# Where the moving operands of the weight products begin in SBUF

## The reference

```
def reference(x, mem, ...):
    x = first_block(x, mem, ...)     # norm @ w_in; pool, rwkv7, differential attention; @ w_out;
                                     # cross-attention to mem; conv FFN 1024 -> 2*2816 -> 1024
    x = second_block(x, ...)         # norm @ w_in; gated spatial unit, top-k attention; merged @ w_o;
                                     # FFN 1024 -> 4096 -> 1024
    return third_block(x, ...)       # 16 meta tokens; norm @ w_in; forgetting attention, gated delta
                                     # rule; @ w_out; conv FFN 1024 -> 2*2816 -> 1024
```

## Time and profile before

| | |
|---|---|
| time, median of 3 runs | 2923.33 us (2919.9 to 2925.94) |
| profiled execution: span from the first to the last instruction | 2921.2 us |
| PE busy | 2791.6 us (96%), 16646 matmul instructions |
| PEld (weight loads) busy | 2339.7 us (80%) |
| DVE (VectorE) busy | 1603.6 us (55%) |
| ACT (ScalarE) busy | 1047.6 us (36%) |
| POOL (GpSimd) busy | 616.9 us (21%) |
| mean granted TensorE clock | 0.974 of full |

### The profile page before, as it was taken

The page is one execution under the profiler, slowest core; times in us unless marked ns, Lnnn a source line. Parts: engine busy times, 40 slices in busy tenths (PEclk is TensorE's granted clock), DMA queues, the critical chain, the costliest instruction groups (busy, mean ns, idle before and its releaser), DMA issues. The chain is left out here.

```text
span 2921.2 us, 42543 instructions
## 1 busy us (share of the span) xinstructions
PE 2791.6 (96%) x16646; PEld 2339.7 (80%) x16646; DVE 1603.6 (55%) x2432; ACT 1047.6 (36%) x1786; POOL 616.9 (21%) x495
## 2 busy tenths in 40 slices
PE   8989999999999999998999999999888998999998
PEld 6769876878888766857788888986777898999986
DVE  5865556365553464934433336975443455576643
ACT  4354343432222323252423224546343233422223
POOL 3430110221100121440100003345454000121101
PEclk9989899999999999989999999999999999999999
DMA  4200221122223321202222222210000122222231
GB/s 157 89 8 8 94 94 58 56 90 94 94 94 98 108 65 66 94 8 80 95 94 94 94 94 73 88 51 2 6 2 1 51 89 78 76 99 92 90 98 61
DMA packets 60307, 210.62 MB, mean 72 GB/s; under 512 B 7926, under 2 KB 8566, under 8 KB 59990
## 3 DMA queue, kind: packets, MB, share of 16 engines
q1 hardware_dynamic: 58934, 207.39, 21.4%
q10 hardware_dynamic: 1184, 0.59, 0.1%
HBM read 205.84 MB, written 2.10 MB: 71 GB/s over the span
## 5 line engine op out<-in xcount | busy, mean ns | idle before, releaser
L272 PE MATMUL ps<-normed_hi,slab_hi 128*128 128x264 f32 (+2 forms) x2568 | 868.6, 338 | 28.0 <-DVE normed_lo L576 13.6
L274 PE MATMUL ps<-normed_hi,slab_lo 128*128 128x264 f32 (+2 forms) x2568 | 852.1, 332 | 0.0
L273 PE MATMUL ps<-normed_lo,slab_hi 128*128 128x264 f32 (+2 forms) x2568 | 851.0, 331 | 0.0
L153 ACT ACTIVATE slab_hi<-ring 128x1024 fp32r<-128x1024 f32 x376 | 397.2, 1057 | 964.3 <-PE ps L274 951.8
L157 DVE TENSOR_TENSOR slab_lo<-ring,slab_hi 128x1024 fp32r<-128x1024 f32 x360 | 479.4, 1334 | 385.0 <-ACT slab_hi L153 384.5
L272 PEld LDWEIGHTS ps<-normed_hi,slab_hi 128*128 128x128 f32 x2568 | 486.0, 189 | 96.4 <-issue 35.0
L273 PEld LDWEIGHTS ps<-normed_lo,slab_hi 128*128 128x128 f32 x2568 | 486.4, 189 | 52.2 <-issue 4.3
L274 PEld LDWEIGHTS ps<-normed_hi,slab_lo 128*128 128x128 f32 x2568 | 484.6, 189 | 49.1
L272 PE MATMUL ps<-hidden_hi,slab_hi 128*128 128x512 f32 x560 | 221.0, 395 | 5.6 <-DVE hidden_lo L223 5.6
L274 PE MATMUL ps<-hidden_hi,slab_lo 128*128 128x512 f32 x560 | 223.0, 398 | 0.0
L273 PE MATMUL ps<-hidden_lo,slab_hi 128*128 128x512 f32 x560 | 221.0, 395 | 0.0
(11 more groups left out here) (579 smaller groups left out, 3951.9 us busy)
## 6 DMA issues: line engine op xcount, KB each, us to landing
ring<-in_stream SPq DMA_DIRECT2D x376, 512.0 KB, 3.3
h<-in_x SPq DMA_DIRECT2D x8, 256.0 KB, 5.8
mix_y<-in_sgu_b SPq DMA_DIRECT2D x1, 1024.0 KB, 6.3
out_features<-ffn_hidden SPq DMA_DIRECT2D x2, 512.0 KB, 3.2
xn<-in_c_recip_count SPq DMA_DIRECT2D x1, 512.0 KB, 3.2
rwkv_a<-in_mem SPq DMA_DIRECT2D x1, 512.0 KB, 4.0
rwkv_b<-in_mem SPq DMA_DIRECT2D x1, 512.0 KB, 4.9
sgu_ln<-in_sgu_ln SPq DMA_DIRECT2D x1, 512.0 KB, 7.8
```

The costliest lines, as they stand in the source:

```text
L153: self.nc.scalar.activation(self.hi[:, n % PARTS, :], self.ring[:, n % SLOTS, :], ACT.Copy).then_inc(self.hi_ready, 1)
L272: nc.tensor.matmul(to, lhsT[0], rhs[0], start=start, stop=False)
L273: nc.tensor.matmul(to, lhsT[0], rhs[1], start=False, stop=False)
L274: return nc.tensor.matmul(to, lhsT[1], rhs[0], start=False, stop=stop)
```

## The change

No instruction is added, taken out or reordered; each engine's program has the same instructions and waits in the same order. What changes is where operands lie. The two parts of an activation are now cut out of one tensor by `spaces`, which adds as many unused bytes in front as are needed to begin at a given place modulo 256. `moving` picks it: 0 for rows of up to 512 columns, and 224 with 576 words (2304 bytes, nine times 256) per row for rows of 528. So all 5832 matmuls of 512 columns that move `normed`, `rows` or `hidden` begin at 0, as the 192 of 256 columns did already; the 5040 of 264 columns begin at 224 (first half) and 0 (second half, since 224 + 1056 is 1280). The last FFN keeps its 512-column rows in the same space, 8 words further, which is 0 again. The 384 that move a slab still begin at 128; their weights (`normed`) began at 160 or 0 and now begin at 0. The small table `gdn_keep` no longer has a buffer, it lies in a part of `wide_v` that is free at the time. Buffers that are opened behind the enlarged ones lie some bytes further.

```diff
+BOUNDARY, WORD = 256, 32
+OPERAND_AT = 0
+WIDE_AT, WIDE = 224, 576
+HIDDEN_AT = (OPERAND_AT - WIDE_AT) % BOUNDARY // 4
...
-        self.hi, self.lo = at or (K.buf(ctx, f"rows_{n}", [P, parts] + shape, F32R) for n in ("hi", "lo"))
+        self.hi, self.lo = at or K.moving(ctx, "rows", [parts] + shape)
...
+    def spaces(self, ctx, name, at, words):
+        self.count += 1
+        skipped = (at - -(-self.nc.sbuf_base // WORD) * WORD) % BOUNDARY
+        both = ctx.enter_context(self.nc.sbuf_tensor(f"{name}_{self.count}", [P, skipped // 4 + 2 * words], F32R))
+        return [both[:, skipped // 4 + n * words:skipped // 4 + (n + 1) * words] for n in range(2)]
+
+    def moving(self, ctx, name, shape):
+        at, pitch = (OPERAND_AT, shape[-1]) if shape[-1] <= S else (WIDE_AT, WIDE)
+        return [laid(x, shape, pitch) for x in self.spaces(ctx, name, at, math.prod(shape[:-1]) * pitch)]
+
+def laid(space, shape, pitch):
+    rows = space[:, 0:math.prod(shape[:-1]) * pitch].rearrange("p (r n) -> p r n", n=pitch)[:, :, 0:shape[-1]]
+    return rows if len(shape) == 2 else rows.rearrange("p (a b) n -> p a b n", b=shape[1])
...
-        self.hi, self.lo = (K.buf(ctx, f"normed_{name}", [P, KT, n], F32R) for name in ("hi", "lo"))
+        self.hi, self.lo = K.moving(ctx, "normed", [KT, n])
...
-        parts = [K.buf(local, f"rows_{x}", [P, PARTS, S], F32R) for x in ("hi", "lo")]
+        parts = K.moving(local, "rows", [PARTS, S])
...
-        parts = [K.buf(local, f"hidden_{x}", [P, PARTS, S], F32R) for x in ("hi", "lo")]
+        parts = K.moving(local, "hidden", [PARTS, S])
...
-        wide_parts = [K.buf(local, f"rows_{x}", [P, PARTS, 2, T3], F32R) for x in ("hi", "lo")]
-        out3 = Residual3(K, K.xn, rows, wide_parts)
-        ffn = Ffn(K, local, "ffn3", rows, 2 * FT, FT, [x[:].rearrange("p n k t -> p n (k t)")[:, :, 0:S] for x in wide_parts])
+        spaces = K.spaces(local, "rows", WIDE_AT, PARTS * 2 * WIDE)
+        out3 = Residual3(K, K.xn, rows, [laid(x, [PARTS, 2, T3], WIDE) for x in spaces])
+        ffn = Ffn(K, local, "ffn3", rows, 2 * FT, FT, [laid(x, [PARTS, HIDDEN_AT + S], 2 * WIDE)[:, :, HIDDEN_AT:] for x in spaces])
...
+        keep = wide_v[0:8, 1, :]
...
-            keep = K.buf(fox, "gdn_keep", [8, T3])
```

More of the change, by code:

```diff
@@ L2 @@
 from contextlib import ExitStack, contextmanager
+import math
 import numpy as np
@@ L2901, in __init__ @@
         self.K, self.gains = K, gains
-        parts = [K.buf(ctx, f"hidden_{x}", [P, PARTS, S], F32R) for x in ("hi", "lo")]
+        parts = K.moving(ctx, "hidden", [PARTS, S])
         rows = Rows(K, ctx, "norm2_g_2", S)
@@ L3066, in decays, with mix_in_3_stage @@
         nc.scalar.activation(heads[:, 1, :], heads[:, 1, :], ACT.Sigmoid)
-def mix_in_3_stage(K, network, fq, fk, fv, gin, wide_heads, keep, causal, scale, factor, ins):
+def mix_in_3_stage(K, network, fq, fk, fv, gin, wide_heads, causal, scale, factor, ins):
     nc = K.nc
@@ L4113, in block_3 @@
             fv = K.buf(fox, "fox_v", [P, NC3, 512])
-            mix_in_3_stage(K, network, fq, fk, fv, gin, wide_heads, keep[:], causal, scale[:], factor[:], ins)
+            mix_in_3_stage(K, network, fq, fk, fv, gin, wide_heads, causal, scale[:], factor[:], ins)
             K.h, K.xn = normed, fq
```

## The result

The changed kernel takes 2936.0 us (median of 5 runs, 2931.26 to 2937.07) against 2923.89 us for the one before: the ratio is 1.0044, with a 95% interval of 1.0032 to 1.0056. It is 12 us slower, where 43 us less were forecast and 2837 to 2918 us were allowed for.

The account below looks back on a forecast made before the run. TensorE was taken as the bound, through the distance between back-to-back products. Savings of 40.5 us (512 columns) and 6 us (264 columns), less 3 us for waits, gave 43.5 us off 2923.3: 2880 us, range 2837 to 2918.

Parts of the forecast that it names:

- The bound and the method: TensorE's back-to-back products set the time; distance per product is window length over the matmul count less two.
- That starts modulo 256 matter: Products of 512 columns: 229 ns from 192, 233 from 160 or 224, so the start costs at least 4 ns.
- 512 columns at 0: Products moving `normed`, `rows`, `hidden`: 225.2 ns each from start 0 (bounds 213.3 to 237.0), saving 40.5 us.
- the boundary is the bad place: Rival: moving start's phase against the weights' start decides; at 237.0 ns from 0, 2945 us; chance 0.07.
- The reason given for 225.2 within the bounds: Weight load gives the surcharge a fixed part, since 264 columns pay 10.8 ns and 512 pay 16 to 20.
- that 256 columns do not foretell: Sign of a wrong prediction: 512 columns from 0 have a price not foretold by 256 columns (118.5 ns).
- 264 columns at 224 and 0: The 5040 half-row products gain 1.2 ns each from the fixed pair of starts, 6 us (−4 to 13).
- The allowance of 3 us for a cover gone: VectorE, feeding slabs and draining PSUM, would be 93 and 94% busy in two stretches; a few waits cost 3 us.
- The 384 products with a moving slab: Moving start stays at 128, weights move to 0; put at 0, 1.5 us either way at 4 ns.
- The rule of the Trainium skill: Warm matmuls follow after N / 2.4 GHz plus about 2.5 ns, through two independent read ports; the change gives 0 us.
- The 215.8 ns of the prediction: The skill pages' distance for 512 columns at any start; if the new start brought it, 92 us instead of 40.5.

Follow-up runs that it names:

- fourth kernel: Kernel before with 512-column operands at 0, but single tensors at 32, 64, 96, 128, 160 or 208 modulo 256, wide rows unmoved; 2906.70 us in one run.

## Why the prediction was wrong

**The bound and the method were right.** TensorE sets the end, no cover was missing, and the loss is in the distance between products. The time of every kernel above follows from those distances to within some 8 us, part of which goes with the granted clock. That starts modulo 256 matter was right too: 229 and 233 ns did belong to the starts (the kernel with all at 192).

**The step that failed: "512 columns at 0".** "If 256 more columns from a boundary add only their own 106.7 ns, 512 columns from 0 take 118.5 + 106.7 = 225.2 ns." They take 232.7. In this term 40.5 us were forecast, and the balance of the 512-column products is nil (the kernel with 512 columns at 0, 0.9985). The error has two parts. The row of 256 columns was no guide to the effect of a start: such products stayed near 119 ns whatever their start was. As means from start to start they took 119.1 ns at 0 with weights at 128, and 119.6 both at 128 with weights at 128 and at 0 with weights at 0, so equal starts even cost half a nanosecond. (That the weight loads, 112 ns, hold them there is likely, but no run shows it.) And I took the boundary of 256 bytes as the thing to be at. What the rows showed was only that two starts out of four seen were cheaper or dearer; every product of before had the same start of weights, so its part could not be seen. That part was named in the rival "the boundary is the bad place" (the phase against weights that begin at 128), with a chance of 0.07. That mechanism, the moving start against the weights' start, is what the runs found, though its price at 0 was 232.7 and not 237.0 ns, just under the 233.1 from which that rival would have decided. The reason given for 225.2 within the bounds, that the weight load makes a fixed part of the surcharge, was not borne out either: loading a half or a quarter of the weight columns left 229.6 to 231.8 ns. The prediction had named the sign, a price of 512 columns from 0 "that 256 columns do not foretell", and it came.

**The second step that failed: "264 columns at 224 and 0".** The pair was timed inside a sequence in which the halves rotate through eight starts, 0.72 us for six. Standing alone, the same pair takes 0.74; it went from the cheapest six of the rotation to a price that none of them had. 6 us of gain were forecast, with bounds of −4 to 13; 11.5 us of loss came. The bounds took in only the rounding of the rows, not that a product's distance depends on what runs ahead of it. The kernel with only the low weights shifted shows the same thing for 512 columns.

**The terms put at little or nothing.** The allowance of 3 us for a cover gone was not called on; nothing got faster. The 384 products with a moving slab, put at 0, went from 233.2 to 232.8 ns in the first stage (means from start to start), which is nothing. With `normed` at 128, where the slab begins, the same products took 228.4 ns: equal starts help with the roles exchanged as well. With the three terms put right, 2880 + 40.5 + 6 + 11.5 − 3 is 2935 us.

**The rule of the Trainium skill** ("TensorE: Matmul & The Clock Gate", "Step-by-step: what each phase is for") that the moving operand and the weights come through ports that do not slow each other disagrees with these runs: the same moving operands take 227.0 or 231.4 ns, depending on where the low part of the weights begins. The 215.8 ns of the prediction were not seen at any start; the least was 226.7. For this change, though, its verdict of no gain was nearer than mine.

**What stays open.** Why equal starts are best, why 192 (64 past the weights) comes second and 128 apart is as slow as 32 apart, and what the 13 ns over the streaming time at equal starts are. They are not the columns loaded, and they are absent at half clock: 213 ns for 256 columns, and 426.9 ns for 512, again 512 / 1.2 GHz, as the mean of eleven distances of the kernel before. Halves of 264 columns that both begin at the weights' start were not tried, since a row of 528 would have to be split in memory.

## What to carry to other kernels

Where float32r products of 512 columns stand back to back, each with a weight load of its own, put the moving operand and the weights at the same address modulo 256. Here that made 233.3 ns into 226.7, and the kernel 1.3% faster than before (2888 against 2924 us). About 29 us of these 36 follow from the distances, by an estimate (6.6 ns for the 4392 products that were at 160, 224 or 64, 2.2 ns for the 912 that were at 192, less the share at half clock). The rest goes with a granted clock of 0.976 to 0.978 in three of its four runs, where the runs of the kernel before had 0.972 to 0.974; the one at 0.973 took 2896 us. For 256 and 264 columns hardly anything was to be had. Judge a start by a long window in which nothing else stands, never by one product in a mixture of starts. And before you extrapolate from rows that differ in one address, ask what all of them have in common: a quantity that never varies in a trace has its effect hidden in every row.

## What the runs showed of the hardware

Products of 512 columns at full clock, by the moving operand's start minus the weights' start, modulo 256; each number is a mean of the distances from start to start over one stage (the fourth kernel is the one with six other starts):

```
difference  ns            read in
0           226.7         hidden, both blocks, weights at 128 and moving at 128; the same with both at 0
32          233.3         kernel before, normed of block 1
64          228.9, 233.3  all operands at 192; rows of block 1 with only the wide rows moved
80          231.2         fourth kernel, normed of block 2 at 208
96          233.3         kernel before, hidden of block 2
128         232.4, 233.3  512 columns at 0; hidden of block 1 at 128 with weights at 0
160         234.2, 234.3  fourth kernel, normed at 32; the change with weights at 0, rows of block 2
192         233.3         kernel before, rows of block 2
224         233.3         fourth kernel, normed of block 1 at 96
```

The step of 256 bytes holds as far as it was met: by the sizes of the tensors in the program, the `hidden` of block 1 and that of block 2 begin at places 256 bytes apart modulo 512 in the kernel with the 512 columns at 128, and both took 226.7 ns.

The single distances repeat in a pattern, which is what sets the mean. At equal starts nearly all are 226 or 227 ns. At a difference of 96 they go 230, 232, 238 ns over the three products of `exact`, at 64 they go 226, 229, 232 (kernel before, `hidden` of blocks 2 and 1). Two patterns were seen at one and the same difference, and what picks one is open. At 128 the `hidden` of block 1 at 128 with the weights at 0 has 229 and 238 ns in turn, 233.3 in the mean; on its timeline on PE, six products from 900.07 take 1.40 us:

```profile
900.07 0.39 PE L275 MATMUL ps<-hidden,slab_hi 128*128 128x512 f32 x1
...
901.47 0.39 PE L275 MATMUL ps<-hidden,slab_hi 128*128 128x512 f32 x1
```

The same difference in the changed kernel gives distances of 228 to 241 ns in a longer round and a mean of 232.4. And in the kernel with only the wide rows moved, the last FFN's operands at 0 took 109.0 / 467 = 233.4 ns on this window of PE:

```profile
2806.00:2915.00 109.00, 109.00 (x469) 1.00 0.21 68
```

where the changed kernel, with the same operands at 0, has 110.0 / 473 = 232.6:

```profile
2805.00:2915.00 110.00, 110.00 (x475) 1.00 0.23 72
```

At 64 `rows` of block 1 took 228.9 ns in the kernel before and 233.3 in the one with only the wide rows moved. At equal starts no second pattern was met.
